# One wait fewer on the weight queue: loads of the gated-MLP stretch and the gathers of expert rows

## The reference

```
for l in 0, 1:
    mp, ms = six modulation vectors each, from silu(c) @ w_ada[l] + b_ada[l]
    h = modulate(rmsnorm(x), shift, scale)
    x = x + gate * (even_mixer(h) if l == 0 else odd_mixer(h))
    h = modulate(rmsnorm(x), shift, scale)
    x = x + gate * moe(h)
y = rmsnorm(x)
```

## Time and profile before

| what | us |
|---|---|
| median of 3 runs | 783.1 |
| lowest and highest of them | 780.12, 784.89 |
| the profiled execution, its own time | 778.97 |
| its span, first to last instruction | 777.2 |

### The profile page before, as it was taken

One profiled execution on the slowest core, in us unless ns is written; L12 is line 12 of the kernel. 1 busy time (PEld: TensorE's weight loads), 2 busy tenths in 40 slices (PEclk: granted clock), 3 DMA queues, 4 the chain that ended last, 5 costly groups with the idle time before them and its releaser, 6 DMA issues.

```text
span 777.2 us, 11354 instructions
## 1 busy us (share of the span) xinstructions
PE 654.4 (84%) x4802; PEld 338.4 (44%) x4802; DVE 226.3 (29%) x554; ACT 158.7 (20%) x313; POOL 32.0 (4%) x76
## 2 busy tenths in 40 slices
PE   4599999999989658999973599999996499997804
PEld 2455656557755323333312455556652233332203
DVE  0412303275522372121100620020525621311026
ACT  3111000144421141111102330131013311111023
POOL 1000000000000010000002000000000100000020
PEclk9899999999999878999988799999998799999857
DMA  8992220569984338999995876443954399999452
GB/s 364 432 432 95 105 99 39 203 290 418 417 358 158 133 125 296 378 413 425 430 425 183 357 307 271 190 169 136 412 230 162 136 366 368 422 429 422 186 190 81
DMA packets 23957, 214.70 MB, mean 276 GB/s; under 512 B 2752, under 2 KB 4576, under 8 KB 12000
## 3 DMA queue, kind: packets, MB, share of 16 engines
q1 hardware_dynamic: 13680, 182.06, 56.8%
q0 software_dynamic: 4320, 15.73, 5.7%
q10 hardware_dynamic: 5904, 16.14, 5.3%
HBM read 199.62 MB, written 14.30 MB: 275 GB/s over the span
## 4 chain that ended last, share of the span: by engine, by line
PE 77%; DMA 10%; DVE 6%; issue 3%; ACT 1%; POOL 1%; SPq 0%; DVEq 0%; ACTq 0%; POOLq 0%
PE bank L1301 28%; PE bank L1534 17%; PE bank L1549 8%; PE bank L1620 5%; DMA ring<-in_ev_in 5%; PE bank L1241 3%; PE bank L1345 2%; DMA ring<-in_ada_w 2%; DMA work<-y_slots,index 2%; PE bank L1438 2%; DVE work L794 2%; PE bank L1515 1%; PE bank L1246 1%; DMA work<-h_all,table 1%; PE bank L1519 1%
## 5 line engine op out<-in xcount | busy, mean ns | idle before, releaser
L1301 PE MATMUL bank<-state,ring 128*128 128x384 f32 x416 | 137.7, 492 | 3.5 <-DMA ring<-in_ev_in 3.5
L1534 PE MATMUL bank<-ring,work 128*32 128x512 f32 x832 | 121.9, 627 | 12.2 <-issue 12.2
L1301 PEld LDWEIGHTS bank<-state,ring 128*128 128x128 f32 x416 | 79.2, 192 | 58.1 <-DMA ring<-in_ev_in 3.7
L1301 PE MATMUL bank<-work,ring 128*128 128x384 f32 x256 | 83.4, 487 | 0.3 <-DVE work L794 0.3
L1301 PEld LDWEIGHTS bank<-work,ring 128*128 128x128 f32 x256 | 48.3, 190 | 34.6 <-DVE work L794 1.4
L1534 PEld LDWEIGHTS bank<-ring,work 128*32 128x32 f32 x832 | 31.3, 115 | 69.5 <-issue 69.5
L1549 PE MATMUL bank<-ring,work 128*32 128x512 f32 x416 | 58.1, 595 | 2.6 <-ACT work L684 2.6
L1128 DVE COPY work<-bank 128x512 f32<-128x512 f32 x18 | 12.4, 691 | 107.6 <-PE bank L1519 107.6
L1534 PE MATMUL bank<-state,work 128*32 128x512 f32 x160 | 43.4, 594 | 0.0
L555 ACT ACTIVATE state<-xT 128x384 f32<-128x384 f32 x40 | 20.6, 521 | 108.9 <-DVE xT L797 95.4
L797 DVE SCALAR_TENSOR_TENSOR xT<-bank,mod,xT 128x128 f32<-128x128 f32 x64 | 22.5, 412 | 67.6 <-PE bank L1301 65.6
(11 more groups left out here) (193 smaller groups left out, 674.5 us busy)
## 6 DMA issues: line engine op xcount, KB each, us to landing
ring<-in_moe SPq DMA_DIRECT2D x24, 2048.0 KB, 15.3
ring<-in_ada_w SPq DMA_DIRECT2D x15, 3072.0 KB, 15.2
ring<-in_moe SPq DMA_DIRECT2D x24, 1024.0 KB, 14.4
ring<-in_ev_in SPq DMA_DIRECT2D x3, 3072.0 KB, 27.2
y_slots<-work ACTq DMA_DIRECT2D x18, 512.0 KB, 9.7
work<-in_moe SPq DMA_DIRECT2D x4, 2048.0 KB, 13.3
state<-in_moe SPq DMA_DIRECT2D x4, 2048.0 KB, 12.5
ring<-in_gm_in SPq DMA_DIRECT2D x4, 2048.0 KB
```

The source lines that it names most:

```text
L1301: mm = pe.matmul(ps[:, 0:T], w[:, k, j * P:j * P + P], x[:, k, :], start=(k == 0), stop=(k == KD - 1))
L1534: mm = pe.matmul(bank[p % 2][rows, :], h_slotT[:, p % 2, k * P + BLOCK * n:k * P + BLOCK * n + BLOCK], held(place_of(e))[:, k * 512:k * 51 ...
```

## The change

SP no longer waits for the gathers ahead of `gm_in 0`. Each load of the stretch waits for its slot alone. POOL's memset that raises `s_sent` stays.

```diff
@@ -396,8 +396,6 @@
 
             def load(*key):
                 kind, i = key
-                if key == ("gm_in", 0):
-                    sp.wait_ge(s_sent, SENT)
                 if BEFORE[key] is not None:
                     wait_used(key)
                 s = HOME[key][0]
```

## The result

| | before | changed |
|---|---|---|
| median of 4 runs, us | 782.35 | 795.07 |
| lowest, highest | 780.12, 784.89 | 791.97, 798.03 |
| span of the profiled execution | 777.2 | 790.1 |

The ratio is 1.0161, 95% interval 1.0111 to 1.0212: 12.6 us slower. The forecast was 794.1. Lines of the changed kernel are two lower than before (L1618 for L1620).

The account below looks back on a forecast made before the run. The end hangs on pass 8's store, the gathers, then `ada 12`'s load. Gathers 14.85 us later less 3.2 won is +11.6, rounded to +11: profiled 778.97 gives 790.0, plus 4.1 for the median, 794.1; range 785 to 800.

Parts of the forecast that it names:

- the 1% that was set as the mark: Whole kernel: a measurement can tell about 1%, 7.8 us, from no change; slower by more had chance 0.74.
- What moves: SP's queue: four loads, 10.49 MB, go earlier; `gm_in 0` at 408.2 instead of 431.1, three from 413.5 instead of 431.5.
- the other signs named: Changed profile: pass 8's store 8 to 12 us, PE's wait some 29 us, DMA above 400 GB/s from 409 to 440.
- The gain, 3.2 us: Before `gm_v`: PE's 3.65 us wait for `ada 12` goes, h is late next; `gm_v` at 447.4 in place of 450.6.
- (1) The store: Store of pass 8 beside loads: 11 us in place of 3.25; first gather at 426.0 in place of 418.2.
- (2) and (3) Bytes left, and the last gather: DMA queues: 4.19 MB of loads and 3.15 MB of gathers left; last gather at 445.7 against 430.85, 14.85 us later.
- (4) From the last gather to h: Last gather to first h tile keeps its 16.5 us; `gm_v` begins at 462.2, +11.6, rounded to +11.
- (5) The clock: PE's granted clock: already at 0.50 while PE stands, so nothing taken; bounds minus 1 and plus 2.
- Even shares: Rival: POOL's and ACT's queues get half the rate; last gather at 437, +3, 786; chance with other partial delays 0.18.
- Loads fill the hole for free: Rival: DMA has room, so stores and gathers land less than 3.2 us later; down to -3.2, 780; chance 0.06.
- Starved gathers: Rival, worst case: gathers move only when the loads are done; +16, 799; chance of worse than +16 was 0.04.
- the first rival: Even shares, which took packets of 4096 B or less literally, so that the queues share about evenly.

Follow-up runs that it names:

- `ada 12` first: Against the kernel before: all four loads still wait for the gathers, but `ada 12` is issued ahead of `gm_in 0`; ratio 0.9971.
- three loads behind the store: Against the kernel before: `gm_in 0` goes with its slot; `ada 12`, `gm_in 1`, `ada 13` wait for the row stores of all passes, not the gathers; ratio 1.0215.
- two early: Against the kernel before: `gm_in 0` and `ada 12` go out with their slots, `gm_in 1` and `ada 13` wait for the gathers; ratio 1.0081.
- two early in 4 KB rows: Against the kernel before: `gm_in 0` and `ada 12` early, cut into 512 KB DMAs with 4 KB rows, the other two behind the gathers; ratio 1.0029.
- three early: Against the kernel before: `gm_in 0`, `ada 12` and `gm_in 1` early, `ada 13` behind the gathers; ratio 1.0107.
- all three with 4 KB rows: Early loads cut to 4 KB rows, against the kernel before: all four, ratio 1.0163; `gm_in 0` and `ada 12`, 1.0029; only `gm_in 0`, 1.0002.

## Why the prediction was right

The time was 795.07 for 794.1 forecast, the ratio clear of no change and, by its interval, over the 1% that was set as the mark. The mechanism was right: the store and the gathers are held by the loads, and the wait for `ada 12` goes. That the number is within 1 us is in part luck, as errors in the steps cancel. Step by step:

- **What moves.** As forecast: `gm_in 0` at 408.13, the others from 413.43, nothing else of SP's. Of the other signs named, PE's wait is 30.07 us for some 29, and DMA moved a mean of 410 GB/s from 409 to 440 where above 400 was expected; the store's 8 to 12 us didn't hold (below).
- **The gain, 3.2 us.** Right in kind: the wait for `ada 12` is gone, and h is late next. It stands by itself in the run with `ada 12` first: 2.6 us by its profile, 2.3 measured, with no change at the edge of the interval. The size is some 0.2 too large: PE waits for h from ACT (L567 in the changed kernel), and before the edit ACT's row at 446.63 (L569, 0.90 us) ends at 447.53, not at the 447.33 of DVE's tile.
- **(1) The store.** Undersized: 11 us taken, 13.21 measured, outside the 8.5 to 11.8 that I had from other stores. The store of pass 7, which took 9.2 us to land (until 418.1), stood ahead in the same queue for longer than I had allowed; the two landed 9.3 us apart. Rounding 11.6 down to 11 "since the store may do better" went the wrong way. With rows of 4 KB in the loads the same store took 7.63. The first gather was 2.15 us later than forecast (428.15 for 426.0).
- **(2) and (3) Bytes left, and the last gather.** 446.7 for 445.7. The sum over bytes held, since nearly the whole of loads, stores and gathers had to pass first. The split was rougher than I had it: of the gathers' 864 packets 91 had moved by 438, and the remainder went at 408 GB/s from 438 to 442, above the 0.37 MB/us that I had taken. A late start and a fast tail cancelled, which is luck.
- **(4) From the last gather to h.** 16.5 us taken, 462.3 - 446.7 = 15.6 measured; the transposes took 4.19 us for 5.29, with the granted clock at 0.63 from 448 to 452 where before it was 0.50 from 432 to 437. `gm_v` began at 462.32 where 462.2 was forecast.
- **(5) The clock.** Nothing was taken for it. It gave 1.1 back there and took some 1.0 in layer 1, where the forecast had a bound of 2.

**The rivals.** *Even shares* was priced wrongly, not only unlikely. I gave it +3, with the gathers' data flowing from 422; when the rows were cut to 4 KB, so that the shares were in fact even (227 packets to 226), the time was +12.8. Its store and its start were priced too early, and its flow a little too fast. I had the data flowing from 422 for 14.8 us, to 437. In the clock of the kernel before, the data of the cut run began between 426.2 and 427.2 (428 to 429, less the 1.76 us by which its pass 8 ended later), the last gather landed at 413.4 + 30.4 = 443.8, and the flow took some 17 us. Of the 7 us between, some 4.7 are the start and 2.3 the flow. *Loads fill the hole for free* falls for four loads, and holds nearly for one of 2.1 MB. *Starved gathers* is closest to what the queues did: the gathers hardly moved until the loads were through. I had it as the worst case at +16, with a tail of 8.5 to 12.6 us after 437.1; the tail was in by 446.7, 8.7 us after 438. With its short tail that rival lands at 445.6, the forecast at 445.7, so the time alone can't tell them apart; the 91 packets can, and they side with the rival. The run with three loads behind the store shows that its +16 can be reached.

What the trace had said of the queues held. The Trainium skill, "DMA: Bandwidth & Descriptors", section "Queues, rings and completion order", lets each engine take a whole packet from one queue and then turn to the next; the counts agree, 94 packets of SP's to 92 of POOL's. Its 4096 B or less by preference ("SWDGE vs HWDGE vs iDMA") stands in the description of what GpSimd builds. POOL's packets, 3.4 KB each in those rows, agree with it; SP's have 14.7 KB, so taking that figure for SP's queue too, as the first rival did, was a step that the section doesn't make.

One thing stays open: why with large rows two early loads and with small rows four come out 1.2 and 2.6 us worse than the start of `gm_v` tells. With small rows the first 48 matmuls of `gm_v` took 22.54 us in place of 20.99, which would be 1.5 of the 2.6, but one profile each is too little for it.

## What to carry to other kernels

Before a prefetch is let go earlier, add up what else the DMA queues must carry between its old and its new place, and who waits for that. Where the path waits for small stores and gathers, bulk loads issued ahead of them held them here until nearly all of the loads had passed, and a wait that looks idle on the weight queue is what keeps the path clear. If one load is late, put that one first among those behind the gate; and for loads that must run beside small transfers, rows cut to the small ones' size are worth a trial: they gave back 4 us with two loads early, nothing clear with one or with four.

## What the runs showed of the hardware that I had not expected

- The first bytes of a gather came later while loads stayed in the queues, whatever their rows. In the changed kernel the first gather was issued at 428.15 and the first packets of POOL's queue fell between 432 and 433. With four loads in 4 KB rows the two were 424.34 and 428 to 429, with three loads behind the store 421.99 and 426 to 427. That is some 4 to 5 us in each. Where SP's queue was empty it was some 1 to 2 us: 418.21 and 419 to 420 in the kernel before, 431.05 and 432 to 433 with two early. And where loads were queued at the issue but ran out, it lay between: 425.96 and 428 to 429 with two early in 4 KB rows, 427.35 and 429 to 430 with three early, whose loads were down to 0.08 MB in that last microsecond. The Trainium skill gives about 1 us to the first byte of a DMA issued from GpSimd ("DMA: Bandwidth & Descriptors", "Latency and other measured facts"); the runs with an empty queue come nearest to it. What the 4 us are was not tried.
- Packets of two queues were counted nearly one for one over 4 us, at 14.7 and 3.4 KB as at 3.5 and 3.7. So the share of the bytes went by the size of the rows.
- TensorE's granted clock came back at different moments after the long stand. The 24 transposes took 4.18 to 5.38 us, without order by how long PE had stood: 4.19 after 30.07 us, 5.38 after 16.85. But they tell what follows. In the four profiles in which they took 5.38 (three early, and all three with 4 KB rows), the granted clock was down again, to a mean of 0.57 to 0.63 over the 4 us in which `gm_v` begins, and its first 48 matmuls took 22.53 or 22.54 us. In the other five changed programs, with 4.18 to 4.73, these took 20.84. The two together make 2.9 us between profiles of this stretch, nearly as much as the gain in question; the time that PE stood doesn't order them, and whether the edits have a part in it isn't shown.
